# Four more expert slots, tokens gathered for four experts at a time, gate rows through DRAM

## What is computed

```python
def trunk_layer(x, cond, p, lam_init, pos, ctx):
    mod = (silu(cond) @ p['w_ada'] + p['b_ada']).reshape(-1, 1, 6 * D_MODEL)
    shift1, scale1, gate1, shift2, scale2, gate2 = jnp.split(mod, 6, axis=-1)
    h = rmsnorm(x, p['norm1']) * (1.0 + scale1) + shift1
    y, own = attention_branches(h, p, lam_init, pos, ctx)   # three mixers, gated, merged, @ w_out
    x = x + gate1 * y
    h = rmsnorm(x, p['norm2']) * (1.0 + scale2) + shift2
    x = x + gate2 * expert_choice_ffn(h, p)
    return x, own

def expert_choice_ffn(h, p):          # 16 experts; each picks its cap = n/8 best tokens
    aff = softmax(xs @ p['w_router'])
    gate, idx = lax.top_k(aff.T, cap)
    xe = xs[idx]
    hg, hu = xe @ p['w_gate'], xe @ p['w_up']               # 1024 x 1024 for each expert
    ye = (silu(hg) * hu) @ p['w_down'] * gate[..., None]
    return zeros.at[idx].add(ye)
```

## Time and profile before

| | us |
|---|---|
| median of three runs | 2066.73 (2064.61 to 2068.13) |
| the profiled execution | 2069.36 |
| its span, first to last instruction | 2067.8 |
| PE busy / share of the span | 1831.0 / 89% |
| DVE, ACT, POOL busy | 504.7, 383.7, 118.1 |
| weights by the hardware DMA queue | 530.03 MB |

### The profile page before, as it was taken

The page is one execution under the profiler, slowest core; times in us unless marked ns, Lnnn a source line. Parts: engine busy times, 40 slices in busy tenths (PEclk is TensorE's granted clock), DMA queues, the critical chain, the costliest instruction groups (busy, mean ns, idle before and its releaser), DMA issues.

```text
span 2067.8 us, 21177 instructions
## 1 busy us (share of the span) xinstructions
PE 1831.0 (89%) x7489; PEld 872.4 (42%) x7489; DVE 504.7 (24%) x1044; ACT 383.7 (19%) x855; POOL 118.1 (6%) x194
## 2 busy tenths in 40 slices
PE   5999999999898887879789999999998979788786
PEld 2654555654432322222245545565544323232222
DVE  2133235323410202010032342342334020020202
ACT  2232222220211010101122322222112111011012
POOL 2221030000000000000012300300000000000000
PEclk8999999999899999999989999999998999999999
DMA  9236322121489999999961482312214999999996
GB/s 335 95 143 268 133 111 72 71 112 41 174 349 423 422 422 423 423 423 422 420 242 67 165 317 90 112 67 77 101 75 157 423 422 422 422 423 423 423 423 266
DMA packets 77638, 537.64 MB, mean 260 GB/s; under 512 B 9168, under 2 KB 9280, under 8 KB 16624
## 3 DMA queue, kind: packets, MB, share of 16 engines
q1 hardware_dynamic: 75024, 530.03, 63.0%
q0 software_dynamic: 2528, 6.49, 1.1%
HBM read 533.31 MB, written 3.18 MB: 259 GB/s over the span
## 4 chain that ended last, share of the span: by engine, by line
PE 70%; DMA 18%; DVE 5%; issue 3%; ACT 2%; SPq 1%; DVEq 0%; ACTq 0%
PE banks L1695 20%; PE banks L1349 12%; PE banks L1332 12%; DMA arena<-in_w_exp 10%; DMA ring<-in_w_exp 7%; PE banks L1371 6%; PE banks L1273 4%; PE banks L1639 4%; PE banks L1308 2%; PE banks L1679 2%; DVE arena L1226 1%; PE banks L1512 1%; PE banks L1459 1%; PE banks L1585 1%; SPq L502 1%
## 5 line engine op out<-in xcount | busy, mean ns | idle before, releaser
L1695 PE MATMUL banks<-ring,arena 128*64 128x512 f32 x2048 | 477.5, 611 | 69.4 <-DMA ring<-in_w_exp 47.6
L1695 PEld LDWEIGHTS banks<-ring,arena 128*64 128x64 f32 x2048 | 143.4, 139 | 394.2 <-issue 264.2
L1695 PE MATMUL banks<-arena 128*64 128x512 f32 x1024 | 229.9, 596 | 29.6 <-ACT arena L852 24.1
L1349 PE MATMUL banks<-arena,ring 128*128 128x384 f32 x768 | 252.7, 487 | 0.0
L1332 PE MATMUL banks<-ring,arena 128*128 128x384 f32 (+1 forms) x768 | 242.3, 477 | 2.3 <-DVE arena L898 2.3
L1349 PEld LDWEIGHTS banks<-arena,ring 128*128 128x128 f32 x768 | 145.1, 190 | 98.9 <-issue 1.5
L1332 PEld LDWEIGHTS banks<-ring,arena 128*128 128x128 f32 x768 | 145.1, 190 | 95.9 <-issue 4.4
L1273 PE MATMUL banks<-arena 128*128 128x128 f32 (+3 forms) x745 | 112.2, 291 | 73.1 <-DVE arena L1220 25.3
L1273 PEld LDWEIGHTS banks<-arena 128*128 128x128 f32 (+3 forms) x745 | 89.2, 147 | 139.3 <-issue 62.1
L1695 PEld LDWEIGHTS banks<-arena 128*64 128x64 f32 x1024 | 71.4, 136 | 167.5 <-issue 141.7
L1217 DVE TENSOR_TENSOR arena<-banks,arena 128x512 f32<-128x512 f32 x32 | 22.1, 692 | 472.9 <-ACT arena L850 472.9
(11 more groups left out here) (197 smaller groups left out, 1282.0 us busy)
## 6 DMA issues: line engine op xcount, KB each, us to landing
ring<-in_w_exp SPq DMA_DIRECT2D x256, 1024.0 KB, 21.5
arena<-in_w_exp SPq DMA_DIRECT2D x128, 1024.0 KB, 23.8
ring<-in_w_att SPq DMA_DIRECT2D x92, 1024.0 KB, 8.0
ring<-in_w_att SPq DMA_DIRECT2D x26, 768.0 KB, 11.2
ring<-in_w_att SPq DMA_DIRECT2D x8, 672.0 KB, 11.4
arena<-in_x_sample SPq DMA_DIRECT2D x1, 1024.0 KB, 8.2
arena<-in_mla_w_uk POOLq DMA_DIRECT2D x2, 512.0 KB, 12.0
arena<-in_mla_w_uv POOLq DMA_DIRECT2D x2, 512.0 KB, 11.8
```

What stands on the lines that cost most here:

```text
L1349: ins = pe.matmul(ps[:, 0:TOK], w[:, k, P * (c % 2):P * (c % 2) + P], hT[:, k], start=k == 0, stop=k == KC - 1)
L1695: ins = pe.matmul(PS[64 * h:64 * h + 64, bank], lhs(k), slots[i][:, c0:c0 + BF], start=k == 0, stop=k == KC - 1)
```

## The change

- `EXTRA` has eight places, so the experts have 16 slots, used in the order `TURN`; unit n of the layer goes to slot `TURN[n % 16]`. Its first seven are three arena slots, two of the ring, one of the arena and one of the ring.
- `gate_rows` is gone. POOL writes the rows of `MODR` to DRAM and reads them back spread over 128 partitions, 1024 KB each, into `G1` and `G2`. The 0.5 goes into the multiplication by `G1`.
- Tokens are gathered for four experts at a time, for group g+1 after gate and up of the second expert of group g. Each chunk is 128 + 64 columns, taken out by ACT (even chunks) or DVE (odd ones), in two instructions, to `XG`; `wide` reads `XG` directly, and `XB`, `DGB` and their copies are gone. The gated matrix of a group is turned (three transposes) at its own place.
- DVE writes `YS` as the product of the bank with `G2`; ACT's copies of it are gone. The combination is added to `X` in one instruction, and the matmuls of its outputs 1 to 5 are 512 wide.
- All `Fori` loops are written out.

```diff
@@ slots
-        EXTRA = [at(15840, SLOT), at(25600, SLOT), at(30720, SLOT), at(0, SLOT)]
+        EXTRA = [at(17888, SLOT), at(19936, SLOT), at(25600, SLOT), at(30976, SLOT),
+                 at(6144, SLOT), at(15840, SLOT), at(3072, SLOT), at(0, SLOT)]
+        TURN = [8, 9, 10, 0, 1, 11, 2, 3, 12, 13, 4, 5, 6, 7, 14, 15]
+        def expert_slot(n):
+            return TURN[n % len(slots)], n // len(slots)
@@ sync
-            with sp.Fori(0, DEPTH) as l:
+            for l in range(DEPTH):
+                jobs_done = [(user_act, evacuated(USER_AT["pv", NJ - 1])), (user_dve, evacuated(USER_AT["br1", KC - 1]))]
+                merged = [(user_dve, evacuated(USER_AT["br2", KC - 1]))]
+                ready = {8: jobs_done, 9: jobs_done, 10: jobs_done, 11: [(rows_out, 4 * 16)], 12: merged, 13: merged,
+                         14: [(user_mm, USER_AT["out", 2, 1] + 1)], 15: [(router_mm, 1)]}
+                for n in range(ALL_EXP):
+                    i, use = expert_slot(n)
+                    sp.wait_ge(used[i].s, used[i].at(l, before[i] + use))
...
+                    sp.dma_start(slots[i], w_exp[l, n // EXP_UNITS, n % EXP_UNITS]).then_inc(filled[i].s, 16)
@@ gpsimd
+                for which in range(2):
+                    for h in range(2):
+                        r = 32 * (2 * which + h)
+                        pool.dma_start(a["gate_rows"][l, which, :, h], MODR[r:r + 2, BF * (1 + which):BF * (2 + which)])\
+                            .then_inc(rows_out.s, 16)
+                pool.wait_ge(rows_out.s, rows_out.at(l, 64))
+                pool.wait_ge(user_act.s, user_act.at(l, evacuated(USER_AT["pv", NJ - 1])))
...
+                pool.dma_start(G1.rearrange("p s n -> p (s n)"), rows[l, 0].to_broadcast([P, 2 * D])).then_inc(g1_in.s, 16)
+                pool.wait_ge(sqd_mm.s, sqd_mm.at(l, 1))
+                pool.dma_start(G2.rearrange("p s n -> p (s n)"), rows[l, 1].to_broadcast([P, 2 * D])).then_inc(g2_in.s, 16)
@@ scalar
-                nc.scalar.mul(G1, PS[:, 0:4, :].rearrange("p (s h) n -> p s (h n)", s=2), 0.5).then_inc(gb_ok.s, 1)
-                nc.scalar.copy(G2, PS[:, 4:8, :].rearrange("p (s h) n -> p s (h n)", s=2)).then_inc(gb_ok.s, 1)
+                def gather_out(g):
+                    for c in range(0, KC, 2):
+                        act.wait_ge(gather_mm.s, gather_mm.in_group(l, g, c + 1))
...
+                        nc.scalar.activation(held_c[:, :, 0:CAP_S],
...
+                        nc.scalar.activation(held_c[:, :, CAP_S:CAP],
@@ vector
+                nc.vector.memset(YS[1], 0.0)
...
+                        if e == 1 and g + 1 < NG:
+                            gather_out(g + 1)
+                            gates(g + 1)
+                        dve.wait_ge(y_mm.s, y_mm.in_group(l, g, e + 1))
...
+                                ins = nc.vector.tensor_tensor(y[32 * e:32 * e + hi - lo, BF * h:BF * h + BF],
+                                                              PS[64 * h + lo:64 * h + hi, 5],
+                                                              G2[64 * h + lo:64 * h + hi, s, BF * h:BF * h + BF], ALU.mult)
...
-                        nc.vector.tensor_tensor(CTMP[:, h], PS[:, 6 + h], G2[:, min(t, 1), BF * h:BF * h + BF],
-                                                ALU.mult).then_inc(comb_ok.s, 1)
-                        ins = nc.vector.tensor_tensor(x, x, CTMP[:, h], ALU.add)
+                        ins = nc.vector.tensor_tensor(x, x, PS[:, 6 + h], ALU.add)
+                        ins.then_inc(comb_ok.s, 1)
@@ tensor
-                gate_rows(l, 0, 0)
-                gate_rows(l, 1, 4)
+                for g in range(NG):
+                    for e in range(GE):
+                        for u in range(4):
+                            if (g, e) == (0, 0):
+                                gather(0, 2 * u)
+                                gather(0, 2 * u + 1)
+                                pe.wait_ge(gather_act.s, gather_act.in_group(l, 0, u + 1))
+                                pe.wait_ge(gather_dve.s, gather_dve.in_group(l, 0, u + 1))
+                            wide(g, e, 0, u, lambda k: held(g, e, k), e % 2, gu_mm)
+                        for u in range(4):
+                            wide(g, e, 4, u, lambda k: held(g, e, k), 2 + e % 2, gu_mm)
+                        if e == 0 and g == 0:
+                            gates_turn(0)
+                        if e == 1 and g + 1 < NG:
+                            for c in range(KC):
+                                gather(g + 1, c)
...
+                        if e == 2 and g + 1 < NG:
+                            gates_turn(g + 1)
```

More of the change, by code:

```diff
@@ L41 @@
 EXP_UNITS = 12
+ALL_EXP = NE * EXP_UNITS
 GE = 4
@@ L375, in backbone, with held @@
         before = [ATT_USES] * SLOTS + [0] * len(EXTRA)
[L376 to L381, removed]
+        rounds = ALL_EXP // len(slots)
+        filled = [sem(f"filled{i}", 16 * (n + rounds)) for i, n in enumerate(before)]
+        used = [sem(f"used{i}", n + rounds, 1) for i, n in enumerate(before)]
+        def expert_slot(n):
+            return TURN[n % len(slots)], n // len(slots)
+        def held(g, e, c):
+            first = c * GE * CAP + e * CAP
+            return XG[g % 2][:, first:first + XW]
         const_in, cond_in, x_in = sem("const_in"), sem("cond_in"), sem("x_in")
@@ L553, in _ @@
             pool.wait_ge(const_in.s, 16)
-            with pool.Fori(0, DEPTH) as l:
+            for l in range(DEPTH):
                 links[0] = 0
@@ L749, in _ @@
             act.wait_ge(x_in.s, 32)
-            with act.Fori(0, DEPTH) as l:
+            for l in range(DEPTH):
                 norm_root(l)
@@ L1021, in _ @@
                                     SIGC.rearrange("p (s k) -> p s k", s=2), ALU.mult).then_inc(cond_ok.s, 1)
-            with dve.Fori(0, DEPTH) as l:
+            for l in range(DEPTH):
                 links[0] = 0
@@ L1112, in _ @@
                     branch(l, ("br2", c))
[L1114 removed]
+                dve.wait_ge(g1_in.s, g1_in.at(l, 16))
                 for t in range(NT):
@@ L1514, in values @@
                 ins.then_inc(user_mm.s, 1)
-            def gate_rows(l, which, bank):
-                for s in range(2):
-                    for h in range(2):
-                        row = 32 * (2 * which + h) + s
-                        ins = pe.matmul(PS[:, bank + 2 * s + h], IDT[:, row:row + 1].to_broadcast([P, P]),
-                                        MODR[:, BF * (1 + which):BF * (2 + which)], start=True, stop=True)
-                        if (s, h) == (0, 0):
-                            settle(ins)
-                ins.then_inc(gb_mm.s, 1)
             for free in (*used, router_mm, at_mm, comb_mm):
@@ L1534, in _ @@
             pe.wait_ge(cond_ok.s, 1)
-            with pe.Fori(0, DEPTH) as l:
+            for l in range(DEPTH):
                 pe.wait_ge(early_in.s, early_in.at(l, 96))
```

311 lines of the change are left out of this document (132 added, 179 removed).

## The result

| | before | after |
|---|---|---|
| median of the runs, us | 2067.4 (2064.6 to 2070.6, four) | 2012.9 (2011.7 to 2013.9, four) |
| ratio | 1 | 0.9736, 95% interval 0.9719 to 0.9752 |
| the profiled execution; its span | 2069.4; 2067.8 | 2011.7; 2009.9 |
| PE busy, share of the span | 1831.0, 89% | 1805.5, 90% |
| hardware DMA queue | 530.03 MB | 530.03 MB |

A forecast was written before the change was run, and what follows sets the result against it. DMA's weight stream was taken to bound the expert stages. Terms 26.0 + 7.1 + 26.0 + 2.5 = 61.6 us off the profiled 2069.36 gave 2007.8; less 2.6 for the median, 2005 us, range 1992 to 2026.

The forecast's parts named there:

- What bounds the kernel: Expert stages: DMA sets the 423 GB/s plateaus and stays the bound, with PE 26 us to spare.
- A unit's worth: Expert stage: every unit in before the stream becomes gapless takes 2.479 us off a layer.
- Units in before the stream: Expert opening: gapless from 567.4 with 19 units in, against 581.0 with 14; 26.0 us in each layer.
- The opening's pace: First expert's units: 6.55 us to the first free slot, then 3.9 each for the next three.
- Gate rows and one-hot: Before the first gather: 3.43 us off for the first pair's gate-row matmuls, 0.8 for DVE's one-hot.
- Start: Kernel start to the end of layer 0's `ada`: a change of 0 was forecast.
- Layer change: Layer 0's last unit to `ada`'s end: 7.1 us off, with the 5.42 us of "issue" taken as the loop's.
- End: Last combination, after layer 1's last unit: 2.5 us off (0 to 4).
- Offset to the median: Whole kernel: the median of the runs was taken to lie 2.6 us below the profiled execution.
- The clock through the opening: Expert opening: PE stays at 1.2 GHz throughout, giving 2024 us; 13%.
- The starved stream in group 0: Gather of group 1 takes 12 us for 7, DMA waits 3 to 5 us a layer: 2011 to 2015; 15%.
- Code: Written-out groups 1 to 3 fetch code anew, some 18 packets a layer; slower above 2.9 us each, up to 2133; 5%.

The follow-up runs named there:

- twelve-slot run: The changed kernel with only four of its eight arena places, so 12 slots instead of 16: 2033.7 us, ratio 0.9840.
- six-matmul run: The changed kernel with six unused 512-column matmuls behind the turns of the affinities, where PE idles under the top-k: 2011.7 us, ratio 0.9743.
- run with added work: The changed kernel with ten unused 512-column matmuls behind the gather of group 1, in group 0's second expert: 2024.1 us, ratio 0.9806.
- sixteen: The changed kernel with 16 unused matmuls behind the last output of `w_out`: 2017.9 us, ratio 0.9751.
- nine: The changed kernel with nine unused matmuls behind `w_out`: 2007.2 us, ratio 0.9708.

## Why the prediction was right, and what of it was not

**What bounds the kernel: right.** 423 GB/s stands from 572 to the layer's end, and work put into group 1 costs nothing. Group 1 takes 109.2 us in after, from the start of group 0's combination to that of its own (660.60 to 769.75), where 107.3 came out of my terms (four experts at 23.0, a gather at 7.0, a group end at 8.3); the next takes 116.6, as PE waits for DMA in it. The stream stays gapless beneath both:

```profile
668.00:777.00 109.00, 99.77 (x473) 37.45 (x472) 24.80 (x41) 8.22 (x17) 0.00 (x0) 1.00 1.01 423
777.00:886.00 109.00, 94.04 (x445) 32.98 (x441) 19.98 (x34) 8.22 (x17) 0.00 (x0) 1.00 1.01 424
```

In 109 us DMA brings 44 units, and PE used 48 in the first of the two: it eats up the filled slots and then waits for the stream, as forecast. A unit's worth by the 358 GB/s of the Trainium skill ("SBUF — State Buffer", "SBUF: two separate sides") would have been 2.93 us by estimate; the trace does not agree, as 424 GB/s stands in the rows of after too, and the twelve-slot run gives 9.7 to 11.7 for four units, 2.4 to 2.9 each. The stream's rate decides for 2.48; the slot run alone would not.

**Units in before the stream: right.** I counted 19 by 567.4. Sixteen slots and 264 GB/s from 554 to 566 (3.0 units), 61 to 568 (0.1) make 19.1 by 568.0. From there 172.9 units at 2.479 end at 996.6, and the last unit's work began 3.8 us after that; the same sum for before (581.0 and 178 units, 1022.3) misses its 1026.16 by 3.9. So the theory gives the difference of the two kernels to 0.1 us. Layer 1's last unit began at 1989.78, 3.7 later than the 1986.1 of my terms: 2.9 of its stage, 1.5 of the layer change and 0.3 carried over, less the 1.0 by which attention gained more than forecast.

**The opening's pace: a term too small.** Forecast were 6.55 us from the gather to the first free slot and 3.9 for each further unit, 18.5 to the fourth; measured 7.15 (553.11 less 545.96), 4.22 and 20.6. The copies are 0.46 + 0.40 us on ACT, where I had 0.36 + 0.3, and I had put the fourth slot free with its unit's own last matmul. The gather began 1.8 us earlier than forecast, the stream became gapless 0.6 later: 2.4 us, which is most of what the 21.8 lost when it came out as 19.7 and 18.9. In layer 0 the two misses cancel: the last unit's work began at 1000.42, forecast about 1000.

**Gate rows and one-hot: both right, with a term left out.** 4.2 forecast, 4.9 and 5.2 measured. The matmuls are worth the 3.4 that they cost when added back, and PE waits 0.98 us for the one-hot where it waited 1.72, 0.7 of the 0.8. Writing the layers out saves 1.4 and 1.0 in attention, which I had at zero. These make 5.5 and 5.1; in layer 0 the granted clock takes 0.6 back (first transposes of 5.9 us for the 5.3 of the run with layers written out).

**Start: missed.** 1.1 us, by the loops: the kernel before with its layers written out has 1.3 there.

**Layer change: a term too large.** 5.6 for 7.1. I had the last unit of `ada` land at +17.4 to +19.8 and took about the middle; the stream allows only the upper end (+19.9, 1020.32). The last eight matmuls then took 1.86 us, with a granted clock of 0.60 from 1020 to 1022; in the six-matmul run they took 1.04 at 0.93, and there the layer change is 20.9 us for after's 21.8. The 7.1 also named the wrong savings: the loop alone gives 5.5, the combination nothing. That the 5.42 us of "issue" belonged to the loop's turn is shown by the run with layers written out; it agrees with what the Trainium skill says of a taken branch to a target outside the pages at hand ("Runtime: NRT & Kernel Launch", "Instruction fetch mechanics"), while no row shows that it is a fetch.

**End: right.** From the last unit's start to the end of DVE's last addition 13.8 us before and 11.4 after, 2.4 of the 2.5. In the chain DVE's two instructions of 0.69 an output gave the pace, and one of them is gone; I had read it off as PE's.

**Offset to the median: wrong.** The profiled execution of before lay 2.6 above its median, and I took these off; that of after lies 1.2 below its own. These 3.8 us and the sum's excess of 3.9 (61.6 against 57.7 in the two profiled executions) are the 7.7 between 2005.2, which I rounded to 2005, and 2012.9.

**Rivals.** The clock through the opening (2024): it was back by the second unit of layer 0 (1.94 us at 555.36), so it costs the opening 2.8 us and not all four units' time. The starved stream in group 0: DMA holds 426 GB/s from 606 to 612, with the 2.3 to 3.5 us of margin that follow from the run with added work, where I had 2. Code: 61 packets of instructions for 50 in the whole execution, three of them from 802 to 921, and the queue of weights beside it without a gap:

```profile
q1 hardware_dynamic: 6913, 50.34, 101.1%
q8 instruction: 3, 0.05, 0.2%
```

PE's 109.2 against 107.3 leaves 1.9 us a group for them if my other terms hold; no run isolates them.

## What to carry to other kernels

Where a stage ends with a gapless stream, count the units landed when the gaps end; each is worth its transfer time, and a microsecond of stall ahead of that point costs one, while behind it there is slack as long as the queue has free slots (here 2.3 to 3.5 us at the gather of group 1, and at least the 8.8 that were added in group 1). Order the first consumers so that copies lie under matmuls: that was worth 8.9 us here for one line, and four slots 21.5. At a stage's change look at what the queue owes first: savings on an engine that waits for it give nothing.

## What the runs showed of the hardware

- PE's granted clock fell from 1.00 to 0.50, which is from 2.4 to 1.2 GHz, after 2.82 us of idling behind 6.7 us of matmuls (six matmuls), but stayed at 1.00 through gaps of 0.8 to 1.0 us where 15.4 us of matmuls stood ahead (sixteen). With 9.3 us ahead (nine) it fell some 3.7 us after them, while PE was at work again between such gaps. What decides was not tested further.
- Writing a loop of two passes out saved 1.3 us at the start and 1.0 to 1.4 us in each attention and expert stage, beside the 5.5 at its turn; 0.7 of one attention stage was the granted clock.
- Attention of the same code took 512.7 and 515.5 us within one execution (nine matmuls), by when the granted clock came back at the layer's start (1.1 us) and by a fall to 0.50 in layer 1 (1.7 us). So a difference of 1 to 3 us between stages of single profiles is to be held against the row of the clock before it is put down to an edit.
- 1024 KB broadcast from DRAM to 128 partitions took 5.9 us from issue to landing (median of four).
